# MLP of a hybrid decoder trunk: the seven weight splits of a unit all on VectorE

## The reference

```python
def squared_relu_mlp(u, w1, w2):
    return jnp.square(jax.nn.relu(u @ w1)) @ w2

for layer in range(DEPTH):
    u = rms_norm(h, norm_mix[layer])
    ...
    h = h + mix
    h = h + squared_relu_mlp(rms_norm(h, norm_mlp[layer]), mlp_w1[layer], mlp_w2[layer])
```

## Time and profile before

| what | value |
|---|---|
| median of 3 runs | 2546.74 us (2543.82 to 2547.41) |
| the profiled execution | 2547.2 us |
| its span, first to last instruction | 2545.2 us |
| mean granted TensorE clock | 0.992 of full speed |
| TensorE busy | 2486.3 us (98%) |
| VectorE busy | 1771.4 us (70%) |
| ScalarE busy | 1116.4 us (44%) |
| GpSimd busy | 1186.1 us (47%) |
| split on VectorE, line 935, from raw weights | 168 of 819 ns mean |
| split on GpSimd, line 1144 | 112 of 1370 ns mean |

### The profile page before, as it was taken

How to read it: one execution, slowest core, us unless ns; L and a number is a source line. 1 busy time by engine, 2 the same in 40 slices (tenths; PEclk the granted TensorE clock), 3 DMA queues, 4 the chain that set the end, 5 groups by cost and what they waited for, 6 DMA issues and landing times. The chain is left out here.

```text
span 2545.2 us, 38274 instructions
## 1 busy us (share of the span) xinstructions
PE 2486.3 (98%) x14136; PEld 2010.4 (79%) x14136; DVE 1771.4 (70%) x2859; ACT 1116.4 (44%) x2150; POOL 1186.1 (47%) x931
## 2 busy tenths in 40 slices
PE   8999999999999999999999999999999999999999
PEld 5778667888887888887877777788788888778887
DVE  6654765477778999873037877676646777899994
ACT  4526654253334444332136666566424333434431
POOL 5362466234445444534215777556423444444441
PEclk8999999999999999999999999999999999999999
DMA  4011003224433643412321112453322344254441
GB/s 173 34 50 34 1 2 120 87 75 153 166 137 108 237 160 137 145 69 97 105 81 57 55 55 76 101 140 88 115 81 87 137 153 166 108 215 157 162 145 66
DMA packets 91711, 275.78 MB, mean 108 GB/s; under 512 B 9879, under 2 KB 39191, under 8 KB 76871
## 3 DMA queue, kind: packets, MB, share of 16 engines
q1 hardware_dynamic: 87976, 255.18, 29.4%
q10 hardware_dynamic: 3552, 18.18, 1.8%
HBM read 197.50 MB, written 73.86 MB: 107 GB/s over the span
## 5 line engine op out<-in xcount | busy, mean ns | idle before, releaser
L1747 PE MATMUL ps<-U_hi,RH 128*128 128x512 f32 x912 | 356.7, 391 | 10.3 <-issue 10.1
L1751 PE MATMUL ps<-U_lo,RH 128*128 128x512 f32 x912 | 356.3, 391 | 0.0
L1752 PE MATMUL ps<-U_hi,RL 128*128 128x512 f32 x912 | 356.1, 390 | 0.0
L1144 POOL TENSOR_TENSOR RL<-RAW,RH 128x512 fp32r<-128x512 f32 x112 | 153.4, 1370 | 380.0 <-ACT RH L827 380.0
L827 ACT ACTIVATE RH<-RAW 128x512 fp32r<-128x512 f32 x280 | 175.4, 628 | 284.6 <-PE ps L1752 277.9
L1747 PE MATMUL ps<-U_hi,W_hi 128*128 128x512 f32 (+2 forms) x656 | 261.4, 399 | 12.9 <-DVE U_lo L3035 11.6
L1752 PE MATMUL ps<-U_hi,W_lo 128*128 128x512 f32 (+2 forms) x656 | 257.9, 393 | 0.0
L1751 PE MATMUL ps<-U_lo,W_hi 128*128 128x512 f32 (+2 forms) x656 | 257.8, 393 | 0.0
L1747 PE MATMUL ps<-SH,RH 128*128 128x512 f32 x656 | 255.4, 389 | 1.0 <-ACT CX L835 0.7
L1752 PE MATMUL ps<-SH,RL 128*128 128x512 f32 x656 | 255.2, 389 | 0.0
L1751 PE MATMUL ps<-SL,RH 128*128 128x512 f32 x656 | 255.2, 389 | 0.0
(11 more groups left out here) (410 smaller groups left out, 6070.8 us busy)
## 6 DMA issues: line engine op xcount, KB each, us to landing
W_raw<-in_pieces SPq DMA_DIRECT2D x30, 1024.0 KB, 5.1
RAW<-in_pieces SPq DMA_DIRECT2D x28, 1024.0 KB, 4.9
RAW<-in_pieces SPq DMA_DIRECT2D x56, 512.0 KB, 8.2
hid_d<-HOA SPq DMA_DIRECT2D x24, 1024.0 KB, 3.9
hid_d<-HOB SPq DMA_DIRECT2D x24, 768.0 KB, 5.4
RHA<-hid_d SPq DMA_DIRECT2D x12, 1024.0 KB, 5.2
RHB<-hid_d SPq DMA_DIRECT2D x12, 768.0 KB, 7.6
U_rawh<-hid_d SPq DMA_DIRECT2D x12, 768.0 KB, 4.7
```

What stands on the lines that cost most here:

```text
L1144: G_.tensor_tensor(ring(RL[i], n), quarter(n, (B22, B11)[i - 5]), ring(RH[i], n).bitcast(F32), ALU.subtract).then_inc(u_lop.sem, 1)
L1747: m = mm(o, a_hi, b_hi, start=first, stop=False, skip_group_check=again)
L1751: mm(o, a_hi, b_lo, start=False, stop=False, skip_group_check=again)
L1752: return mm(o, a_lo, b_hi, start=False, stop=last, skip_group_check=again)
```

## The change

GpSimd's `unit_low` is gone; VectorE's `unit_low` takes the quarters of splits 5 and 6 too, and one semaphore counts all seven splits of a unit. GpSimd keeps the four sums of a unit, and three splits of hidden blocks at the turn (line 1151). On VectorE, split 5 stands behind split 4; in the down stage each of splits 0 to 5 of the next unit follows a collect as before. Split 6 of a unit stands at the head of the next step: ahead of split 0 of the following up unit, and in the down stage behind the first product's collect of the unit itself. SP waits on the one semaphore, 7 per unit.

```diff
--- before.py
+++ after.py
@@ -326,7 +326,6 @@
         u_add = Again(l_sig, 8)
         u_hi = Again(l_tanh, 4)
         u_lod = Again(l_exp, 4)
-        u_lop = Again(l_ix, 4)
         f_up = Again(l_aa, 4)
         f_copy = Again(l_t2, 4)
         f_hid = Again(l_mult, 4)
@@ -421,7 +420,7 @@
         def unit_ready(L, n, i):
 
             w = N_W * L + n
-            return u_lod.at(5 * w + i + 1) if i < 5 else u_lop.at(2 * w + i - 4)
+            return u_lod.at(7 * w + i + 1)
 
         def stored(L, u):
 
@@ -931,7 +930,7 @@
                 dve.wait_ge(*u_hi.at(7 * w + i + 1))
                 if i == 2:
                     dve.wait_ge(*u_add.at(4 * w + 4))
-                src = ring(RT[i], n) if i in (1, 2) else quarter(n, (B11, None, None, B21, B12)[i])
+                src = ring(RT[i], n) if i in (1, 2) else quarter(n, (B11, None, None, B21, B12, B22, B11)[i])
                 V_.tensor_tensor(ring(RL[i], n), src, ring(RH[i], n).bitcast(F32),
                                  ALU.subtract).then_inc(u_lod.sem, 1)
 
@@ -1037,7 +1036,9 @@
             unit_low(0, 3)
             unit_low(0, 4)
             comb_low(3)
+            unit_low(0, 5)
             for u in range(N_UP - 1):
+                unit_low(u, 6)
                 unit_low(u + 1, 0)
                 if u:
                     hidden_sums(u - 1)
@@ -1045,9 +1046,9 @@
                     unit_low(u + 1, i)
                 for i in range(3):
                     hidden_out(u, i)
-                    if i < 2:
-                        unit_low(u + 1, i + 3)
+                    unit_low(u + 1, i + 3)
             hidden_sums(N_UP - 2)
+            unit_low(N_UP - 1, 6)
             for i in range(2):
                 unit_low(N_UP, i)
                 sub_low(0, 2 * i)
@@ -1067,6 +1068,7 @@
             for i in range(1, 4):
                 sub_low(1, i)
             unit_low(N_UP, 4)
+            unit_low(N_UP, 5)
             dve.wait_ge(*q_lo.at(sub_no(L, 1, 3)))
             collect(0, 0)
             hidden_sums(N_UP - 1)
@@ -1077,7 +1079,9 @@
                         dve.wait_ge(*f_back.at(32 * (L + 1)))
                     if d or i:
                         collect(d, i)
-                    if 1 <= i <= 5 and d + 1 < N_DOWN:
+                    if i == 0:
+                        unit_low(N_UP + d, 6)
+                    elif d + 1 < N_DOWN:
                         unit_low(N_UP + d + 1, i - 1)
                     if i and d + 2 < N_DOWN:
                         sub_low(d + 2, i - 1)
@@ -1133,16 +1137,9 @@
                 pool.wait_ge(*ring_free(L, n, 2))
                 G_.tensor_tensor(ring(RT[2], n), R[B12], R[B11], ALU.add).then_inc(u_add.sem, 1)
                 pool.wait_ge(*u_add.at(4 * w + 3))
-                pool.wait_ge(*u_lod.at(5 * w + 1))
+                pool.wait_ge(*u_lod.at(7 * w + 1))
                 G_.tensor_tensor(R[B11], R[B21], ring(RT[2], n), ALU.subtract).then_inc(u_add.sem, 1)
                 pool.wait_ge(*u_add.at(4 * w + 4))
-
-            def unit_low(n, i):
-
-                w = N_W * L + n
-                pool.wait_ge(*u_hi.at(7 * w + i + 1))
-                G_.tensor_tensor(ring(RL[i], n), quarter(n, (B22, B11)[i - 5]), ring(RH[i], n).bitcast(F32), ALU.subtract
-                                 ).then_inc(u_lop.sem, 1)
 
             def sub_low(i):
 
@@ -1152,11 +1149,9 @@
 
             for n in range(N_W):
                 unit_sums(n)
-                unit_low(n, 5)
                 if n == N_UP:
                     for i in range(4, 7):
                         sub_low(i)
-                unit_low(n, 6)
             p0 = (P_MLP0, P_MLP1)[L]
             for j in range(2):
                 pool.wait_ge(split_hi, p0 + 2 + j + 4)
@@ -1182,8 +1177,7 @@
             def load_unit(n):
 
                 if n >= 2:
-                    sp.wait_ge(*u_lod.at(5 * (N_W * L + n - 1)))
-                    sp.wait_ge(*u_lop.at(2 * (N_W * L + n - 1)))
+                    sp.wait_ge(*u_lod.at(7 * (N_W * L + n - 1)))
                 if n < N_UP:
                     dma(RAW8[n % 2][:], pieces[M_PIECE[L] + 4 + 2 * n].rearrange("p (k c) -> p k c", k=KC)).then_inc(u_in[n % 2].sem, 16)
                     return
@@ -1326,8 +1320,7 @@
                 load(0, p)
             mlp_sp(sp, load, 0)
             sp.wait_ge(hl, 2 + 8)
-            sp.wait_ge(*u_lod.at(5 * N_W))
-            sp.wait_ge(*u_lop.at(2 * N_W))
+            sp.wait_ge(*u_lod.at(7 * N_W))
             sp.wait_ge(*f_res.at(2))
             with sp.Fori(0, 2) as t:
                 for j in range(4):
```

## The result

| what | before | with the change |
|---|---|---|
| median | 2544.96 us (2541.98 to 2547.41, 6 runs) | 2556.32 us (2555.57 to 2564.49, 6 runs) |
| the profiled execution; its span | 2547.2; 2545.2 us | 2556.0; 2554.2 us |
| mean granted TensorE clock | 0.992 | 0.993 |

The ratio is 1.0049, with a 95% interval of 1.0037 to 1.0061: slower by more than 0.2%, by 11.4 us between the medians. The forecast was 2559 us, 2549 to 2568. It started from 2547.2 us for the kernel before; the six runs give 2544.96, so what compares with the 11.4 is its difference, 12.2.

What follows compares the result with a forecast made beforehand. TensorE was taken as busy throughout both 160 us MLP stages, with VectorE nearly full in the down stage. Turn delays 4.2 + 4.6 plus clock 3.4 made 12.2 us on 2547.2, 2559.4, less 0.5: 2559 us, range 2549 to 2568.

Steps and rivals of the forecast that it cites:

- step 3: TensorE's third product of the second down unit, at the turn, starts later: +4.2 us in layer 0, +4.6 in layer 1.
- Up stage, nothing: Up stage of the MLP: the subtractions moved to VectorE fall into its idle time and cost nothing.
- Down stage, steady, nothing with 0.4 us left: Steady down stage: VectorE's 1.20 us more per unit cost nothing; split 0 keeps 0.4 us before GpSimd's next sum.
- overflow: Rival, down stage: VectorE reaches split 0 over 0.4 us later than counted; 8.8 us on top, 2568 us; chance 11%.
- Step 1: Turn, layer 0: split 6 ends late behind the hidden sums, so SP's weights load goes out at 832.4, not 827.23.
- T: Time SP issues the third down unit's weights load at the turn: 832.4 in layer 0, 2238.5 in layer 1.
- Step 2: Turn: the reloaded H lands at T + 20.5 (852.9) in layer 0, T + 21.3 (2259.8) in layer 1.
- Step 4: Behind the new stop at the turn, TensorE's granted clock falls to 0.50: +1.7 us per layer, 3.4 in all.
- Nothing behind the turn gives it back: After the turn, none of the 12.2 us lost is regained, as TensorE is busy throughout.
- The reload stays hidden: Rival, turn: split 6 gets the port first and the store overtakes the weights; +1.4 us, 2548 us; chance 14%.
- VectorE is simply full: Rival, down stage: VectorE at 98% pays for every added instruction; 29 us, 2576 us; chance 3%.
- Faster: Rival, turn: first stop 1.0 us shorter per layer, clock doesn't fall, H no later; 5.4 us won, 2541; chance 3%.

Runs made afterwards that it cites:

- Experiment 1: The changed kernel with split 6 of the first down unit moved ahead of the four hidden sums on VectorE; 2544.54 us, ratio to before 0.9996.
- experiment 2: The changed kernel with SP's load of the third down unit's weights moved behind the hidden store and the reload of H; 2547.96 us, ratio 1.0007.
- experiment 3: The kernel before, with SP's load of the third down unit's weights waiting for the last hidden sum, no split moved; 2555.58 us, ratio 1.0044.
- experiment 4: The kernel of Experiment 1, with split 6 of each of the other 13 down units made twice on VectorE; 2555.8 us, ratio 1.0038.
- experiment 5: The changed kernel with both the early split 6 of Experiment 1 and the SP order of experiment 2; 2549.28 us, ratio 1.0014.
- experiment 6: The kernel of Experiment 1, with GpSimd's three splits of hidden blocks at the turn moved to VectorE too; 2544.93 us, ratio 0.9998.
- kernel 7: The kernel of experiment 6 with the hidden sums earlier at the turn and SP reloading H ahead of the weights; 2544.54 us, ratio 1.0.

## Why the prediction was right

It was: slower by 11.4 us, 12.2 forecast, for the reason given. Experiment 1 takes the late split away, experiment 2 the load's place in the queue, and with either the loss goes; experiment 3 makes the load late by itself, and most of the loss comes. That the sum is so close is in part luck, as step 3 shows.

- **Up stage, nothing:** right. VectorE has 118.5 of 160 us and TensorE no stop.
- **Down stage, steady, nothing with 0.4 us left:** right, and the margin is there. The timelines of VectorE and GpSimd in a down unit show split 0 behind the first sum, as counted:

```profile
973.16 0.92 DVE L934 TENSOR_TENSOR RL<-RAW,RH 128x512 fp32r<-128x512 f32 x1
```

```profile
972.23 1.29 POOL L1133 TENSOR_TENSOR RT<-RAW 128x512 f32<-128x512 f32 x1 [12.55 <-PE ps L1745]
973.60 1.62 POOL L1135 TENSOR_TENSOR RAW<-RAW 128x512 f32<-128x512 f32 x1
```

  Split 0 starts at 973.16, 0.44 us ahead of the second sum at 973.60, so it still comes first. The rival "overflow" needed more than that; experiment 4 shows a loss of that kind, with 0.72 us more per unit, but by a collision with the first sum.
- **Step 1, T:** 831.80 for 832.4, with the collision counted (1.78 us). The sums ended 1.1 us earlier than before, not 0.5: behind the shorter first stop (3.97 us) the granted clock was back at 826.35, not at 826.96, so it took nothing of what the restart gained. In layer 1, whose MLP began 4.7 us later than before, T is 2241.93 - 4.7 = 2237.2 for 2238.5, 1.3 early for the same reason.
- **Step 2, H** (by the start of its collects): T + 22.3 in layer 0 for T + 20.5, and T + 20.9 in layer 1 for T + 21.3. The term that was mis-sized is what the weights cost the store: 4.8 - 1.3 - 1.4 = 2.1 us in the sum, 3.3 and 3.0 us by SP's wait from the store's issue to the reload's (10.2 and 10.0 us, before 6.9 and 7.0). That the weights cause it is shown: the wait is 10.4 and 9.7 us in experiment 3, which has them 1.3 us ahead too, and 6.7 to 7.1 where they go 3.7 us ahead or more, or behind H (before and experiments 1, 2 and 5). The rule of the Trainium skill cited there ("DMA: Bandwidth & Descriptors", Queues, rings and completion order), that on each DMA engine one ring's descriptors are consumed in ring order, agrees with all of these. If weights and store shared the engines, the store would be late too; no run tells the two apart. The rest is the reload: 10.9 us from issue to H in layer 0, before 10.2, and 9.7 in layer 1, before 10.9.
- **Step 3, the third product:** +5.3 us in layer 0 (854.97 for 849.57, start of the MLP +0.1) where +4.2 was forecast, and +2.9 in layer 1 (2263.68 for 2256.08, less 4.7) where +4.6 was. One came out 1.1 us high and the other 1.7 low; that they cancel, 8.2 for 8.8, is luck.
- **Step 4, the clock:** 2.7 and 1.4 us for 1.7 each, 4.1 for 3.4, as what is left of 8.0 and 4.3 us. The two falls were of 6.83 and 3.41 us; by the starts of their matmuls they cost 2.7 and 1.5.
- **Not foreseen:** the stop of 1.0 us per layer at the first unit's fifth product. It cost nothing that can be seen here, since H set the later time.
- **"Nothing behind the turn gives it back":** true of the MLPs (12.3 for 12.2), not of the execution: 3.3 us lay in falls of the clock between the MLPs, which differ from one execution to the next; the medians, 11.4 us apart, lie nearer to the sum.
- **The rivals:** "The reload stays hidden" fails: GpSimd's sum got the port first, and the store did not overtake the weights. "VectorE is simply full" falls with experiment 1, and so do its 2576 us. They were also what the first half of the Trainium skill's rule on offloading ("Perfetto Trace Analysis", Optimizing Scalar/DVE Operations) would have made of the time; this case, with 2544.54 us for kernel 1, sides with its second half. "Faster" was right that the port binds the chain to the first stop (experiment 6). But kernels 1 and 6, whose first stops are 1.1 and 4.2 us shorter than before, are not faster beyond the noise.

## What to carry to other kernels

When a producer moves to another engine, look at every queue whose next entry waits for it. Split 6 had some 10 us of slack (done at 831.78, for a product that starts at 841.58), but the store behind its load on SP had none, and the reload behind the store had, before the change, 0.56 us in layer 0 and none in layer 1. Here the loss was undone by moving one instruction or one load, not by giving the work back. And where one engine has no idle time over a seam, as VectorE in kernel 7, each new order here only brought up the next wait. That its work at the seam would have to shrink is a guess that no run here tests.

## What the hardware showed that was not expected

- After stops of about the same length the granted clock was 0.50 for 3.41 us or for 6.83. Behind the first stop of 5.05 us it was 6.83 in both layers before, and 3.41 in both layers of experiment 3. Behind that of 3.97 us it was 3.41 in both layers of the changed kernel, and in kernel 1 it was 3.41 in layer 0 and 6.83 in layer 1. Kernel 7 has the same stop of 2.5 us in both layers, with a fall of 3.41 in layer 0 and none in layer 1. Those worked out above lost 1.5 to 2.7 us each. Such falls go with much of the spread between executions: of the 21 runs of the kernel before that belong to experiments 1 to 4, the one of 2542.88 us has a mean granted clock of 0.995, the one of 2555.11 us has 0.989. So a profiled pair can differ by 3 us outside of what was changed.
- The same 1 MB of weights cost the store behind it nothing if issued 3.7 us ahead or more (SP's wait for it 6.8 to 7.1 us, and 6.7 without them), and some 3 us if issued 1.3 us ahead (9.7 to 10.4).
